# PEER routing on one core: 136 candidates per head in place of 256, smaller index tables, half heads ranked in pairs

## The reference

```python
s1 = jnp.einsum('nhd,kd->nhk', q[..., :half], k1).astype(jnp.float32)
s2 = jnp.einsum('nhd,kd->nhk', q[..., half:], k2).astype(jnp.float32)
v1, i1 = lax.top_k(s1, PEER_TOPK)
v2, i2 = lax.top_k(s2, PEER_TOPK)
cand = (v1[..., :, None] + v2[..., None, :]).reshape(PEER_CHUNK, PEER_HEADS, PEER_TOPK * PEER_TOPK)
sc, ci = lax.top_k(cand, PEER_TOPK)
e = (jnp.take_along_axis(i1, ci // PEER_TOPK, axis=-1) * PEER_NKEYS
     + jnp.take_along_axis(i2, ci % PEER_TOPK, axis=-1))
g = jax.nn.softmax(sc, axis=-1)
act = jax.nn.gelu(jnp.einsum('nhkd,nd->nhk', u_tab[e], hc).astype(jnp.float32))
return jnp.einsum('nhk,nhkd->nd', (g * act).astype(hc.dtype), v_tab[e])
```

## Time and profile before

| what | value |
|---|---|
| median of 3 runs | 1959.97 us (1957.33 to 1962.45) |
| the profiled execution, its own time | 1958.85 us |
| its span, first to last instruction | 1957.2 us |
| TensorE busy | 1513.6 us, 77% |
| VectorE busy | 1184.0 us, 60% |
| GpSimd busy | 641.3 us, 33% |
| ScalarE busy | 340.0 us, 17% |
| mean granted TensorE clock | 0.781 |
| DMA | 669.61 MB, of it 546.87 on GpSimd's queue |
| the chain that ended last | DMA 33%, TensorE 24%, VectorE 9%, issue 7% |

### The profile page before, as it was taken

One profiled execution on the slowest core, in us unless ns is written; L12 is line 12 of the kernel. 1 busy time (PEld: TensorE's weight loads), 2 busy tenths in 40 slices (PEclk: granted clock), 3 DMA queues, 4 the chain that ended last, 5 costly groups with the idle time before them and its releaser, 6 DMA issues.

```text
span 1957.2 us, 22286 instructions
## 1 busy us (share of the span) xinstructions
PE 1513.6 (77%) x7491; PEld 681.5 (35%) x7491; DVE 1184.0 (60%) x2942; ACT 340.0 (17%) x846; POOL 641.3 (33%) x746
## 2 busy tenths in 40 slices
PE   7999999999978888867788676765666566666676
PEld 6577866476934454422344211110101011110111
DVE  7653255224857777555778984478985455454545
ACT  5451346202322222011201010010000000000001
POOL 3501134002832233323233333333333333333332
PEclk9989999999978889976888866566665656566655
DMA  6325632747699999999999999999999999999996
GB/s 203 118 77 140 200 121 77 301 162 235 229 404 421 412 411 410 420 412 411 421 393 397 413 406 412 414 420 416 405 400 422 411 414 414 416 416 414 412 422 288
DMA packets 141477, 669.61 MB, mean 342 GB/s; under 512 B 17268, under 2 KB 50228, under 8 KB 71412
## 3 DMA queue, kind: packets, MB, share of 16 engines
q0 software_dynamic: 75648, 546.87, 68.3%
q1 hardware_dynamic: 65716, 121.33, 18.1%
HBM read 661.00 MB, written 19.65 MB: 348 GB/s over the span
## 4 chain that ended last, share of the span: by engine, by line
DMA 33%; PE 24%; DVE 9%; issue 7%; POOL 3%; ACT 1%; DVEq 0%; POOLq 0%
DMA uv<-in_peer_uv,idxT 21%; DMA w_out<-in_peer_uv,idxT 11%; PE ex_acc L2604 10%; PE ex_hb L2498 4%; PE ro_pq L2069 3%; DVE uv L2772 2%; POOL uv L2389 2%; PE ex_late L2523 1%; PE ro_ps L2045 1%; DVE w_out L2772 1%; POOL w_out L2389 1%; PE ex_late L2571 1%; DVE ch_iu L1828 1%; PE ex_late L2538 1%; DVE ch_ci L1828 1%
## 5 line engine op out<-in xcount | busy, mean ns | idle before, releaser
L2498 PE MATMUL ex_hb<-ffn_gain,spread 24*128 24x512 bf16 x1040 | 350.4, 497 | 396.4 <-DVE uv L2772 262.5
L2772 DVE SCALAR_TENSOR_TENSOR uv<-uv,ex_hb 128x1024 f32<-128x1024 f32 x344 | 416.6, 1220 | 313.5 <-DMA uv<-in_peer_uv,idxT 281.2
L2389 POOL DMA_INDIRECT uv<-in_peer_uv,idxT x340 | 322.1, 947 | 595.7 <-PE ex_acc L2604 517.6
L2498 PEld LDWEIGHTS ex_hb<-ffn_gain,spread 24*128 24x128 bf16 x1040 | 54.3, 99 | 730.3 <-DVE uv L2772 391.0
L2772 DVE SCALAR_TENSOR_TENSOR w_out<-w_out,ex_hb 128x1024 f32<-128x1024 f32 x176 | 213.3, 1219 | 154.1 <-DMA w_out<-in_peer_uv,idxT 127.6
L2604 PE MATMUL ex_acc<-uv,wts 128*32 128x512 f32 x1376 | 275.8, 945 | 0.0
L2389 POOL DMA_INDIRECT w_out<-in_peer_uv,idxT x172 | 161.9, 941 | 308.6 <-PE ex_acc L2604 267.3
L2923 ACT ACTIVATE ex_gelu<-ex_dots 128x4 f32<-128x4 f32 (+1 forms) x131 | 26.9, 205 | 955.9 <-DVE uv L2772 647.3
L2604 PE MATMUL ex_acc<-w_out,wts 128*32 128x512 f32 x704 | 144.0, 953 | 0.0
L2604 PEld LDWEIGHTS ex_acc<-uv,wts 128*32 128x32 f32 x1376 | 47.5, 147 | 160.1 <-issue 160.1
L2571 PE MATMUL ex_late<-hx,sgT 128*128 128x264 f32 x256 | 67.3, 421 | 0.0
(11 more groups left out here) (553 smaller groups left out, 2077.0 us busy)
## 6 DMA issues: line engine op xcount, KB each, us to landing
sgT<-in_late_w SPq DMA_DIRECT2D x24, 1024.0 KB, 9.1
uv<-in_peer_w_q SPq DMA_DIRECT2D x15, 1024.0 KB, 8.3
gate_ring<-in_w_in SPq DMA_DIRECT2D x6, 2048.0 KB, 10.0
uv<-in_peer_uv,idxT POOLq DMA_INDIRECT x344, 13.7
ks_rows<-in_ks_pages SPq DMA_DIRECT2D x64, 64.0 KB, 2.2
vs_rows<-in_cache_v_sel SPq DMA_DIRECT2D x64, 64.0 KB, 2.1
gate_ring<-in_kc_pages SPq DMA_DIRECT2D x64, 64.0 KB, 2.1
de_ks<-ks_rows SPq DMA_DIRECT2D x8, 512.0 KB, 9.9
```

The lines of the kernel that those rows point to most:

```text
L2389: pool.indirect_dma_start(slot(s).rearrange("p j n -> p (j n)"), None, table, bass.IndirectOffsetOnAxis(ap=S.idxT[:, t:t + 1], axis=0))\
L2498: last = pe.matmul(hb[s % 2][:, CHUNK * h:CHUNK * h + CHUNK], spread[p, k % LOAD, :], h_rows[p, l % 2, CHUNK * h:CHUNK * h + CHUNK], start ...
L2772: dve.scalar_tensor_tensor(out=rows_, in0=rows_, scalar=1.0, in1=hb[s % 2][:], op0=ALU.mult, op1=ALU.mult, accum_out=dots[:, B % 2, c:c + ...
```

## The change

Of the 16 x 16 sums of a head only 136 are built: all 16 partners for the best eight of the first half, and for the other eight of the first half only the best partner. The table of the first half has 8 entries for the place; the second has 24: 16 numbers of the second half, and 8 finished expert numbers (first half times 128 plus the best of the second) for the other sums. A place of 128 or more is split so that the first look-up finds nothing and the second finds the finished number; `iota` gets the values 128 to 135 behind 0 to 15 for that.

In the route half heads are ranked in pairs except the last two. The first tile's 16 jobs all come ahead of the second tile's 16, so there are 32 jobs and 16 chunks of weights. GpSimd looks up heads 0 to 5 in portions of 1, 2, 2 and 1 heads, VectorE heads 6 and 7 alone. The second tile's projection comes after job 11, its additions and its scaling stand together on VectorE ahead of half head 12, and the numbers are transposed after job 19. The order of rooms is changed, so that gather 4 takes the scores' room and gathers 5, 6 and 7 the slots of chunks 12, 13 and 14. The expert stage takes over the smaller candidates and tables; its order stays.

```diff
+FULL = TOPK // 2
+CANDS = FULL * TOPK + TOPK - FULL
+SECOND = TOPK + FULL
+FIELDS = TOPK + SECOND
...
-ROOMS = (3, 0, ROOM_S, 1, 2, ROOM_HT, ROOM_H, ROOM_REST)
+ROOMS = (ROOM_S, 0, 1, 2, 3, ROOM_HT, ROOM_H, ROOM_REST)
...
-        self.fi = sb("fi", [P, 2 * GROUP, TOPK])
+        self.fi = sb("fi", [P, 3, FIELDS])
         self.work = sb("work", [P, 2 * GROUP + 3, TOPK * TOPK])
-        self.cand = self.work[:, 0:GROUP].rearrange("p h (a b) -> p h a b", b=TOPK)
-        self.hit = self.work[:, GROUP + 3:].rearrange("p h (a b) -> p h a b", b=TOPK)
+        flat = self.work[:].rearrange("p h n -> p (h n)")
+        self.cand = flat[:, 0:2 * CANDS].rearrange("p (h n) -> p h n", h=2)
+        self.pool_hit = flat[:, 2 * TOPK * TOPK:2 * TOPK * TOPK + 2 * TOPK * SECOND]
+        self.hit = flat[:, (GROUP + 7) * TOPK * TOPK - TOPK * (SECOND + GROUP):]
...
+        self.iota = sb("iota", [P, SECOND])
...
-    cube = [m, count, TOPK, TOPK]
+    cube = [m, count, FULL, TOPK]
     to = eg[:, 1, first * TOPK:(first + count) * TOPK]
-    link(dve.tensor_tensor(cand, v[:, :, 0, :].unsqueeze(3).broadcast_to(cube),
-                           v[:, :, 1, :].unsqueeze(2).broadcast_to(cube), ALU.add))
-    best16(dve, link, [(R.sc[0:m, h, :], R.ci[0:m, TOPK * h:TOPK * h + TOPK],
-                        R.cand[0:m, h].rearrange("p a b -> p (a b)")) for h in range(count)])
+    dve.tensor_tensor(cand[:, :, 0:FULL * TOPK].rearrange("p h (a b) -> p h a b", b=TOPK),
+                      v[:, :, 0, 0:FULL].unsqueeze(3).broadcast_to(cube), v[:, :, 1, :].unsqueeze(2).broadcast_to(cube), ALU.add)
+    link(dve.tensor_tensor(cand[:, :, FULL * TOPK:], v[:, :, 0, FULL:],
+                           v[:, :, 1, 0:1].broadcast_to([m, count, TOPK - FULL]), ALU.add))
+    best16(dve, link, [(R.sc[0:m, h, :], R.ci[0:m, TOPK * h:TOPK * h + TOPK], cand[:, h, :]) for h in range(count)])
...
+def places(dve, hl, ci):
+
+    dve.tensor_scalar(hl[:, 0], ci, 4, None, ALU.logical_shift_right)
+    return dve.tensor_scalar(hl[:, 1], ci, FULL * TOPK + TOPK - 1, None, ALU.bitwise_and)
+
+
+def choose_index(dve, link, R, t, head, eg, m=P):
+
+    f = R.fi[0:m, 0]
+    hl, hf, pick = (x[0:m, :, 0:TOPK] for x in (R.hl, R.hf, R.pick))
+    dve.tensor_copy(f[:, 0:2 * TOPK], R.iu[0:m, t, 2 * head:2 * head + 2, :].rearrange("p w a -> p (w a)"))
+    link(places(dve, hl, R.ci[0:m, 0:TOPK]))
+    dve.scalar_tensor_tensor(out=f[:, 2 * TOPK:], in0=f[:, FULL:TOPK], scalar=float(NKEYS),
+                             in1=f[:, TOPK:TOPK + 1].broadcast_to([m, TOPK - FULL]), op0=ALU.mult, op1=ALU.add)
+    link(dve.tensor_copy(hf, hl))
+    for j, (first, last) in enumerate(((0, FULL), (TOPK, FIELDS))):
+        n = last - first
+        over = [m, TOPK, n]
+        hit = R.hit[0:m, 0:TOPK * n].rearrange("p (k a) -> p k a", a=n)
+        link(dve.tensor_tensor(hit, hf[:, j].unsqueeze(2).broadcast_to(over), R.iota[0:m, 0:n].unsqueeze(1).broadcast_to(over),
+                               ALU.is_equal))
+        link(dve.tensor_tensor(hit, hit, f[:, first:last].unsqueeze(1).broadcast_to(over), ALU.mult))
+        link(dve.tensor_reduce(pick[:, j], hit, AX_X, ALU.add))
+    return dve.scalar_tensor_tensor(out=eg[:, 0, head * TOPK:head * TOPK + TOPK], in0=pick[:, 0],
+                                    scalar=float(NKEYS), in1=pick[:, 1], op0=ALU.mult, op1=ALU.add)
...
-    PORTIONS = ((0, 2), (2, 2), (4, 2), (6, 1), (7, 1))
-    SPLIT = 14
-    JOBS = [(hh, 0, 1) for hh in range(SPLIT)] + [(hh, 0, 2) for hh in range(SPLIT, HH)] + [(hh, 1, 2) for hh in range(SPLIT)]
+    PORTIONS = ((0, 1), (1, 2), (3, 2), (5, 1))
+    ALONE = (HEADS_P - 2, HEADS_P - 1)
+    JOBS = [(hh, 0, 1) for hh in range(HH)] + [(hh, 1, 2) for hh in range(HH)]
     kept_by = [sum(b - a for _, a, b in JOBS[:j]) for j in range(len(JOBS) + 1)]
-    OUT_AT, SQUARE_AT, ROOT_AT = 7, 9, 10
-    TURN_AT = 12
-    SHARED = HEADS_P - 2
-    EXP_AT, CHOICE_AT = 23, 24
+    OUT_AT, SQUARE_AT, ROOT_AT = 11, 12, 12
+    TURN_AT = 14
+    EXP_AT, CHOICE_AT = 18, 19
     LATE_AT = 11
...
+            for i, (first, count) in enumerate(PORTIONS):
                 pool.wait_ge(E["halved"], i + 1)
                 n = count * TOPK
+                f = R.fi[:, 1:1 + count]
                 hl, hf, pick = (x[:, :, TOPK:TOPK + n] for x in (R.hl, R.hf, R.pick))
+                link(pool.tensor_copy(f[:, :, 0:2 * TOPK],
+                                      R.iu[:, 0, 2 * first:2 * (first + count), :].rearrange("p (h w) a -> p h (w a)", w=2)))
                 pool.tensor_copy(hf, hl).then_inc(E["places_read"], 1)
+                link(pool.tensor_scalar(f[:, :, 2 * TOPK:], f[:, :, FULL:TOPK], float(NKEYS), None, ALU.mult))
+                link(pool.tensor_tensor(f[:, :, 2 * TOPK:], f[:, :, 2 * TOPK:],
+                                        f[:, :, TOPK:TOPK + 1].broadcast_to([P, count, TOPK - FULL]), ALU.add))
                 pool.wait_ge(E["places_read"], i + 1)
+                for j, (a0, a1, sums) in enumerate(((0, FULL, (4, 2)), (TOPK, FIELDS, (12, 6, 3)))):
+                    width = a1 - a0
+                    terms = R.pool_hit[:, 0:n * width].rearrange("p (k a) -> p k a", a=width)
+                    hit = terms.rearrange("p (h k) a -> p h k a", h=count)
+                    link(pool.tensor_tensor(terms, hf[:, j].unsqueeze(2).broadcast_to([P, n, width]),
+                                            R.iota[:, 0:width].unsqueeze(1).broadcast_to([P, n, width]), ALU.subtract))
                     link(pool.tensor_scalar(terms, terms, 0.0, None, ALU.is_equal))
+                    link(pool.tensor_tensor(hit, hit, f[:, :, a0:a1].unsqueeze(2).broadcast_to([P, count, TOPK, width]),
                                             ALU.mult))
+                    for w in sums:
                         link(pool.tensor_tensor(terms[:, :, 0:w], terms[:, :, 0:w], terms[:, :, w:2 * w], ALU.add))
+                    if j:
+                        link(pool.tensor_tensor(terms[:, :, 0], terms[:, :, 0], terms[:, :, 2], ALU.add))
+                    link(pool.tensor_tensor(pick[:, j], terms[:, :, 0], terms[:, :, 1], ALU.add))
...
-            used = {BATCH: 2 * 12, BATCH + 1: 2 * 13, BATCH + 3: 2 * 14}
+            used = {BATCH + 1: 2 * 13, BATCH + 2: 2 * 14, BATCH + 3: 2 * 15}
...
-                if c == 8:
+                if c == 10:
...
-                    pe.wait_ge(E["indexed"], len(PORTIONS) - 2)
-                    pe.wait_ge(E["numbered"], 1)
+                    pe.wait_ge(E["indexed"], len(PORTIONS))
+                    pe.wait_ge(E["numbered"], len(ALONE))
...
-                if j == HH - 2:
+                if j == TURN_AT + 2:
                     split_high(1)
                 if j == EXP_AT:
-                    act.wait_ge(E["shifted"], len(PORTIONS))
+                    act.wait_ge(E["shifted"], len(PORTIONS) + len(ALONE))
...
+            def best(hh, count=1):
+                dve.wait_ge(E["s_kept"], kept_by[hh + count - 1] + 1)
+                best16(dve, link, [(R.v[:, 0, x, :], R.iu[:, 0, x, :], s[:, x, :]) for x in range(hh, hh + count)])
+
+            def choose(i):
+                first, count = PORTIONS[i]
+                n = count * TOPK
+                choose_best(dve, link, R, 0, first, count, E["shifted"], R.eg)
+                if i:
+                    dve.wait_ge(E["places_read"], i)
+                places(dve, R.hl[:, :, TOPK:TOPK + n], R.ci[:, 0:n]).then_inc(E["halved"], 1)
+
+            def choose_alone(head):
+                choose_best(dve, link, R, 0, head, 1, E["shifted"], R.eg)
+                choose_index(dve, link, R, 0, head, R.eg).then_inc(E["numbered"], 1)
...
+            best(0, 2)
+            choose(0)
+            best(2, 2)
+            best(4, 2)
+            choose(1)
+            best(6, 2)
+            best(8, 2)
+            choose(2)
+            best(10, 2)
+            choose(3)
+            add(2)
+            add(3)
+            variance(1)
+            scale(1)
+            dve.wait_ge(E["iota"], 2)
+            best(12, 2)
+            choose_alone(ALONE[0])
+            best(14)
+            best(15)
+            choose_alone(ALONE[1])
```

More of the change, by code:

```diff
@@ L1952, in _ @@
             pool.memset(S.idxT[:, TOK:], 0.0).then_inc(E["qz"], 1)
-            pool.iota(R.iota[:], [[1, TOPK]], base=0, channel_multiplier=0,
-                      allow_small_or_imprecise_dtypes=True).then_inc(E["iota"], 1)
+            for first, n, value in ((0, TOPK, 0), (TOPK, TOPK - FULL, FULL * TOPK)):
+                pool.iota(R.iota[:, first:first + n], [[1, n]], base=value, channel_multiplier=0,
+                          allow_small_or_imprecise_dtypes=True).then_inc(E["iota"], 1)
             pool.memset(S.wts[:], 0.0)
@@ L1961, in _ @@
             link = own(pool, E["pool_own"])
-            pool.wait_ge(E["iota"], 1)
-            for i, (first, count) in enumerate(PORTIONS[:-1]):
+            pool.wait_ge(E["iota"], 2)
+            for i, (first, count) in enumerate(PORTIONS):
```

(28 more changed lines are left out.)

76 lines of the change are left out of this document (removed).

## The result

The changed kernel takes 1970.7 us (median of 15 runs, 1965.7 to 1976.3), the kernel before, timed beside it, 1959.8: a ratio of 1.0063, 95% interval 1.0053 to 1.0073. It is slower by about 11 us. The forecast was 1967 with a range of 1954 to 1974 and slower as the likeliest sign; the time lies in the range, 3.7 above the point. The profiled execution took 1976.3 us with a span of 1974.7 and is the slowest of the fifteen, so in the two profiles the difference is larger, 17.4. One later execution of this kernel (of again_timed) took 2028.1 us at a mean granted clock of 0.701, where the others have 0.766 or more; its time and its profile are left out.

The account below looks back on a forecast made before the run. From 540 us the DMA gather stream bounds: its start, MB sharing the queues, dry spells; compute sets the pace between 596 and 713. Terms of +6.8 us took 1958.85 to 1965.7 profiled, 1967 as median (1.1 above); range 1954 to 1974.

Parts of the forecast that it names:

- Job 28 would be due at 541.5 and waits until 551: TensorE, end of the route: job 28 stands idle for chunk 14 of the query weights until it lands at 551.
- So chunk 14 ends just behind them: DMA queues: chunk 14, issued at 529.3 beside gathers 0 to 6, ends at 550 and has landed at 551.
- the sum: The prediction's addition of its terms along the timeline, from ranking at 471.0 to +6.8 us at the end.
- Row 19: Expert stage, VectorE: its existing 3.1 us wait for this gathered row absorbs 3.1 of 13.6 us lateness, leaving 10.5.
- The hole in DMA: Between 553 and 567: DMA idles some 8 us because later gathers need job 29 or the stage's end.
- As if one small packet went after each large one: DMA queues: a load's 1 KB packets alternate with 8 KB gather packets, taken as 0.37 us per packet.
- the ranking on VectorE: Route: VectorE's work, started at 471.0, is done at 525.3, ahead of GpSimd's end at 526.8.
- Portions of 1, 2, 2 and 1 heads: 12.8: Route, VectorE: choices for heads 0 to 5 take 12.8 us, at 3.9 per two heads and 2.5 per one.
- rival 3: Route: expert numbers are not earlier, GpSimd needing 530 or more; everything shifts by 3 to 5 us: 1971. Chance 0.10.
- shorter choices in the dips: Expert stage: in later DMA dips, like that at 1050, shorter choices on VectorE give back perhaps 1.3 us.
- rival 2: Expert stage: chunk 14 lands in time and shorter choices, 15 us on VectorE, fill most dips: 1952. Chance 0.13.
- Rival 1: DMA queues: last chunks are not held up, chunk 14 lands by 542, stage ends about 551: 1957.5. Chance 0.22.

Follow-up runs that it names:

- again_timed: The changed kernel unaltered, timed again beside the kernel before: ratio 1.0079 (1.0062 to 1.0096).
- early_split: The changed kernel with second tile's VectorE work earlier, transposes after job 24, and ScalarE's two first-tile split copies one job earlier each: 1958.0 us, ratio 1.0007.
- choice_padded: The changed kernel with second tile's VectorE work earlier, transposes after job 24, and two more maxima in every expert-stage choice: ratio 0.9994 (0.9993 without the maxima).

## Why the prediction came out as it did

**The mechanism was right, and most of its terms.** "Job 28 would be due at 541.5 and waits until 551", 9.5 us: the wait was 9.75. "So chunk 14 ends just behind them", 21.6 us after its issue: it was 23.0. From landing to the first expert matmul the sum had 12.5 us (551 to 563.5, though its own terms, 10.5 and 1.7, make 12.2); it took 12.52 (557.42 to 569.94). From there to the first freed slot 12.8; measured 12.74. Row 19 was to absorb 3.1 us; it absorbed 2.7, as the lateness of the gathers fell from 19.7 to 17.0 there. The hole in DMA was forecast for 553 to 567 with some 8 us of idle time; next to nothing moves from 560 to 566, and the queues are not full again until 590.

"As if one small packet went after each large one" is what the queues do: 148 beside 149 packets. The rule of the Trainium skill that I had weighed against it (DMA: Bandwidth & Descriptors, section Queues, rings and completion order), a whole packet of typically 9 to 17 descriptors drained per turn, would by the prediction's estimate with 17 have brought the chunk in after some 13 us. With 9 (from norm_final the prediction had read about eight) it would have taken some 21 us, an estimate from the page's figure (seven turns, each behind the 2.6 us of a gather and with some 0.4 of its own), and the counts would be the same, since a gather has nine packets per engine, eight of 8 KB and a short one. So the counts alone don't decide; the times of the single packets do. From 538 to 551 there are 578 packets of 8 KB. In the 4 ns up to the end of such a packet one of 1 KB begins in 537 cases, and another of 8 KB in 74, as many as 100 or 200 ns later by chance (99 and 74). With no load on the queues, from 575 to 590, another of 8 KB begins there in 543 of 638 cases. So the turns are of one packet each here, as the profile counts packets, and the rule with 9 or more does not describe this case in these units.

**The term that was mis-sized: the ranking on VectorE.** The sum had it done at 525.3 and GpSimd last at 526.8. GpSimd's last addition ended at 527.2, near the forecast by luck: it began 1.7 us later than in the sum (478.58) and waited 0.85 for VectorE, and its portions together were 2.0 shorter than the 49.8. VectorE ended at 530.3:

```profile
530.10 0.17 DVE L1880 SCALAR_TENSOR_TENSOR ch_eg<-ch_pick 128x16 f32<-128x16 f32 x1
...
526.99 0.22 POOL L2003 TENSOR_TENSOR ch_eg<-ch_pick 128x16 f32<-128x16 f32 x1
```

Ranking began at 470.84 for the 471.0 of the sum, pairs took 3.0 for 2.97, the two heads done alone 6.1 and 6.05 for 6.05. What was over are the four portions: 4.5, 4.7, 5.7 and 3.1, together 18.0 us instead of "Portions of 1, 2, 2 and 1 heads: 12.8". Six single operations make up 5.1 of the 5.2: the addition at 473.85 (2.26 for 0.29), and these:

```profile
484.70 0.97 DVE L1850 TENSOR_TENSOR ch_work<-ch_v 128x16 f32<-128x16 f32 x1
...
495.09 0.73 DVE L1848 TENSOR_TENSOR ch_work<-ch_v 128x256 f32<-128x256 f32 x1
495.75 0.79 DVE L1850 TENSOR_TENSOR ch_work<-ch_v 128x16 f32<-128x16 f32 x1
...
499.85 0.98 DVE L1860 TENSOR_SCALAR ch_hl<-ch_ci 128x32 uint32<-128x32 uint32 x1
...
506.07 0.71 DVE L1853 TENSOR_TENSOR ch_eg<-ch_sc 128x16 f32<-128x16 f32 x1
```

Undisturbed they take 0.15, 0.42, 0.15, 0.17 and 0.18 (the 0.15 is that of 128x8; no undisturbed one of 128x16 is in the trace). Each ran beside a GpSimd operation of 0.7 to 2.2 us. early_split shows it for the first and largest; for the others it was argued from the times alone. The trace of before had it already, beside a GpSimd operation that ran from 514.33 to 515.60 and then undisturbed:

```profile
514.51 1.38 DVE L1842 TENSOR_TENSOR ch_work<-ch_v 128x256 f32<-128x256 f32 x1
...
522.61 0.42 DVE L1842 TENSOR_TENSOR ch_work<-ch_v 128x256 f32<-128x256 f32 x1
```

So the slowing could have been read, and priced, ahead of the run. The Trainium skill (SBUF — State Buffer, section SBUF: two separate sides) says that VectorE, in its two-port modes or with two SBUF inputs, and a GpSimd operation that reads SBUF lock a shared pair of ports, and that the loser waits for the whole instruction; the 2.26 beside 2.13 agrees. One of the six does not: the addition at 495.75 ended at 496.5, 1.3 us ahead of the GpSimd operation beside it (495.63 to 497.81), and no run shows why. The maxima and index searches between them, at 0.28 to 0.30, were not stretched.

So the condition of rival 3 was met, on the engine that it did not name: not GpSimd but VectorE needed until 530. It was priced at 3 to 5 us on top of the forecast and 1971 us, which is what came out. The forecast and rival 3 were not alternatives, and I had treated them as such: the chance of both together belonged in the sum. From the late numbers follow the other shifts: transposes at 530.42 instead of 526.9, chunk 14's issue 4.9 later than in the sum (another 1.7 because TensorE, after waiting 2.62 us for the numbers, ran job 21 in 3.63 instead of 1.95), and the first freed slot at 582.7 instead of 576.3.

**The lateness hardly fell, and the dips gave nothing back.** The sum let compute win back 5.5 us by 713 and took 1.3 us for shorter choices in the dips. At 713 the gathers were 15.0 us late where 8.1 was forecast; the decay from 19.9 is 4.9, near the 5.5 of the sum. But it didn't last: 17 us from 775 to the end. The gathers were issued a little less late for a while, but the bytes that they moved were not. From 560 to 590 the changed kernel's queues moved 7.5 MB, those of before 12.6; the last third of that stretch, of the kernel before and then of the changed one:

```profile
580.00:590.00 10.00, 6.63 (x40) 3.49 (x36) 8.46 (x25) 3.44 (x5) 3.81 (x4) 1.00 1.02 421
```

```profile
580.00:590.00 10.00, 10.00 (x40) 4.96 (x36) 4.40 (x16) 1.88 (x3) 3.74 (x4) 0.63 0.91 349
```

5.1 MB are 12 us at the 0.42 MB per us of full queues; chunks 14 and 15, moved behind the start of the gathers, are 5 more, and the gathers' earlier start gives 2 back. These 15 us, an estimate from the windows, stood by 600, and from then on the queues were as full as before (419 GB/s for 421 from 600 to 650, 412 for 412 from 650 to 700), so there was little left to win back: from 596 to 713 the sum let compute set the pace, where the full queues did. The dips are about as deep as before (0.84 at 990, 0.84 at 1070, 0.90 at 1140, for 0.87, 0.82 and 0.89), and choice_padded shows that the choices don't fill them. With that rival 2 falls too. Rival 1 fell with the 23.0 us of chunk 14.

Both errors point the same way and make 17 us out of 6.8 in the profiles: the first slots came free 6.3 us later than in the sum, and of the 6.8 us that it then let the lateness lose, only some 2.5 were lost. By the profile, on which the sum was built, the forecast is off by 10.6 us. The timed runs lie lower, at 12 and 15 by their ratios; that the median came within 4 us of the forecast is in part luck, by a share of the time that no profile shows.

## What to carry to other kernels

When two streams share the DMA queues, ask in which order their last transfers are issued, and count packets, not bytes: here a late load in small packets was held up until the large ones ran out, and the work that needed it stood idle. Price a move by every transfer that it leaves behind; a gain of 2 us at the first gather came with a held-up load, a late end of the stage and a hole. When a stream has stood still and its queues are full again, count the bytes that it lost; a compute stage that catches up behind it doesn't bring them back. And when work is spread over VectorE and GpSimd at the same time, the sum of the undisturbed durations is a lower bound: find a place in the trace where both work at once and take the durations from there.

## What the runs showed of the hardware

- Packets of a load and of gathers alternated one for one (148 to 149, and 150 to 153, per 3 us), whether they had 1 KB or 8 KB: 1 MB in 1 KB pieces took 23 to 24 us beside gathers and 7.0 in the median of all such loads of the changed kernel.
- A load issued in the same moment as the first gather landed in 5.5 us; one issued 3 us after it took 24. The load's first packet moved 1.0 us after its issue and that of the gather issued with it after 4.1, so a few us decide.
- A VectorE addition of 128x128 with two inputs took 2.26 us beside a GpSimd operation of 2.13, and 0.29 when 0.11 us of that was left. One of 128x16 took 0.79 beside one of 2.18 and ended 1.3 us ahead of it.
